# Encoder layer on one core: order of the first units, of the gates' rows and of two loads per head

## The chip, the cores and the metric

The kernel runs on 1 core of one Trainium2 chip. Times are device microseconds of that core for one execution of the whole program. TensorE's clock has two levels, 1.2 and 2.4 GHz; the profile gives the granted clock as a share of the higher one.

## The reference

One hybrid encoder layer on x of 1024 x 2048 (float32): RMSNorm, one input projection, eight heads of dilated sliding-window attention and four heads of a bidirectional mLSTM, gates, one output projection into the residual. Cut to what matters:

```python
h = _rmsnorm(x, norm_w)
proj = jnp.einsum('bsd,df->bsf', h, w_in)          # 2048 -> 8208 columns
q_a, k_a, v_a, z_a, q_m, k_m, v_m, o_m, z_m, g = jnp.split(proj, offsets, axis=-1)
qa = _rope_partial(_rmsnorm(q_a, q_norm_w), cos, sin)
ka = _rope_partial(_rmsnorm(k_a, k_norm_w), cos, sin)
# three (window, dilation) patterns per head, mixed by their softmax denominators
attn = dilated_attention(qa, ka, v_a) * jax.nn.silu(z_a)
# mLSTM forward and backward, with gates i, f from g; running-max stabiliser
h_fwd = _mlstm_chunkwise(qm, km, vm, i_fwd, jax.nn.log_sigmoid(f_fwd))
h_bwd = flip(_mlstm_chunkwise(flip(qm), flip(km), flip(vm), flip(i_bwd), flip(jax.nn.log_sigmoid(f_bwd))))
hm = jax.nn.sigmoid(o_m) * _rmsnorm(h_fwd + h_bwd, m_norm_w) * jax.nn.silu(z_m)
y = jnp.concatenate([attn, hm], axis=-1)
out = x + jnp.einsum('bsf,fd->bsd', y, w_out)
```

## The kernel before

The input projection is done by groups of 2 x 2 blocks with seven products instead of eight (a Strassen-Winograd scheme). A group takes one half of the 2048 inputs and a pair of column tiles; there are NG = 64 groups, so 448 units of one product each, then 128 units of the output projection. A product is 12 matmuls of 128 x 512: both sides are split into a rounded high half (float32r) and the rest as a low half, and high x high, low x high and high x low are added up in one PSUM bank.

The weights' side of a product is a block of w_raw or a sum s_tmp of blocks (s_one, s_two, s_three, s_four on VectorE). ScalarE rounds it (weight_hi, L978), VectorE subtracts to get the low half (weight_lo, L1214), two units ahead of TensorE. The x side are seven operands: B11, B21, B22 scaled by norm_w, and T1 = B12 - B11, T2 = B22 - T1, B22 - B12 (third sum) and B21 - T2 (fourth). They are built once for each of three stages, from four blocks of x in the arena: ScalarE casts the high half t_hi, VectorE makes the low half t_lo. For stage 0 this happens at the start of the program: x_block loads, scale_x on ScalarE, B11 scaled on VectorE after its low half, t_one and t_two on VectorE, t_three and t_four on GpSimd.

Each engine runs one list of instructions, in order, written as a loop over the units u; inside a unit every helper adds its part in a fixed order, and engines meet only by semaphores. On VectorE a unit is: softmax_dve of the heads, evict of the previous product, weight_lo of the block two units on, the x sums at the start, gates_and_norm, mlstm_dve, attention_dve, and the next group's weight sums. SyncE's list issues nearly all loads and stores; its waits stand in the same order, so a load waits behind the waits of the loads before it, among them those for s_done in next_weights. GpSimd's list issues the accumulating stores and the loads and stores of the turned rows (turned_rows).

The gates: in units 9 to 40 a small product is streamed, from unit 41 on VectorE turns it into rows (scans in units 53 to 55), and in units 59 to 64 it copies eight stripes of 32 x 1024 into rows, li and m. SyncE stores rows at unit 66, TensorE transposes at 67, ScalarE and VectorE read at 68 and 69. The first reader is the mLSTM; a wait for all of it stands at unit 92 in SyncE's list.

An attention head h starts at unit 357 + 18 h and spans some 26 units; "at" counts from its start. SyncE loads the raw q and k at -4, the quarter of rows that is rotated at 2, v at 4, the norms as broadcasts at 5 and 6, z at 6. VectorE rotates at 4 and 5, GpSimd stores the result to rot_dram and loads it back into the raw rows in another layout (4 to 6), VectorE waits for it and multiplies by the norms at 8 and 9 (normed, L1576). v is multiplied by xrs at 7 (L1624), z at 10 (L1621). TensorE makes scores from 10, transposes v at 11 and the first probabilities at 12 (L928); these wait for v's transposes having been copied out of PSUM, half by ScalarE, the rest by VectorE at 12 (L1649, L1652), the last statement of attention_dve. Heads 5 to 7 run mostly in the output units, where VectorE evicts a product by L1668.

Of the kernel before, what the change touches and what calls it, by code (L numbers as in the profile page):

```python
# [112 lines left out]
def build_program(nc, xT, w_all, w_gates, vecs, norm_cols, m_cols, att_mask, rope, eye, tri, fin, part, y_dram, t_dram, eps_dram, rows_dram, rs_dram,  # L113
                  rot_dram, outT):
    with ExitStack() as ctx:
# [270 lines left out]
        def _(sp):  # L386
# [46 lines left out]
            def gate_stores(u):  # L433
                if u == 48:
                    sp.wait_ge(x_cols, 7)
                    sp.dma_start(eps_dram, spread1[0:2 * TB, 0, :]).then_inc(rows_out, 16)
                if u == 66:
                    sp.wait_ge(g_dve, GD_ROWS)
                    for k in range(4):
                        sp.dma_start(rows_dram[k], rows[32 * k:32 * k + M_HEADS, :]).then_inc(rows_out, 16)  # L440
# [85 lines left out]
            def attention_loads(h, at):  # L526
# [38 lines left out]
                if at == 4:  # L565
                    if h > 0:
                        sp.wait_ge(a_pv, 4 * h)
                    tile_done(sp, g[0], 0)
                    sp.dma_start(halves(v_at), fin_tile(g[0], 0)).then_inc(v_raw, 16)
                if at == 6:  # L570
                    if h > 0:
                        sp.wait_ge(a_out, 16 * h)
                    tile_done(sp, g[1], 1)
                    sp.dma_start(halves(ystage), fin_tile(g[1], 1)).then_inc(z_raw, 16)
# [49 lines left out]
            for kt in range(KP):  # L624
                x_block(0, B11, kt)
            weights(0, 1, 0, 0)
            weights(0, 1, 1, 1)
            for kt in range(KP):
                x_block(0, B12, kt)
            weights(0, 0, 1, 4)  # L630
            for kt in range(KP):
                x_block(0, B22, kt)
# [70 lines left out]
        def _(pe):  # L703
# [64 lines left out]
            def gates_and_norm(u):  # L768
# [26 lines left out]
                if u == 67:  # L795
                    pe.wait_ge(g_dve, GD_ROWS)
                    for b in range(2 * TB):
                        src = (gr[3] if b < TB else gr[1])[0:64, (b % TB) * P:(b % TB + 1) * P]
                        t = nc.tensor.transpose(ps[:, 4 + b // TB, (b % TB) * 64:(b % TB + 1) * 64], src, ident[0:64, 0:64])
                    t.then_inc(g_pe, 1)  # L800
# [172 lines left out]
        def _(act):  # L973
# [19 lines left out]
            def scale_x(b, blk):  # L993
                for kt in range(KP):
                    if blk == B11:
                        act.wait_ge(b11_in[kt], 16 * (b + 1))
                    else:
                        act.wait_ge(b_in[blk], 16 * KP * (b + 1))
                    at = 8 * (b % 2) + 4 * (blk in (B21, B22)) + kt
                    nc.scalar.activation(stage[blk][:, kt, :], stage[blk][:, kt, :], ACT.Copy, scale=ncol[:, at:at + 1]  # L1000
                                         ).then_inc(pre[blk], 1)
# [30 lines left out]
            def gates_and_norm(u):  # L1032
# [30 lines left out]
                if u == 68:  # L1063
# [104 lines left out]
            for kt in range(KP):  # L1168
                act.wait_ge(b11_in[kt], 16)
                nc.scalar.activation(t_hi[:, 0, kt, :], stage[B11][:, kt, :], ACT.Copy, scale=ncol[:, kt:kt + 1]  # L1170
                                     ).then_inc(th_done[0], 1)
            weight_hi(1)
            scale_x(0, B12)
            for u in range(UNITS):
# [6 lines left out]
                if u == 0:  # L1181
                    scale_x(0, B22)
# [19 lines left out]
        def _(dve):  # L1202
# [133 lines left out]
            def gates_and_norm(u):  # L1336
# [75 lines left out]
                if u == 59:  # L1412
                    g_step(nc.vector.tensor_copy(rows[0:32, :], t[0:32, :]))
                if u == 60:
                    g_step(nc.vector.tensor_copy(rows[32:64, :], t[32:64, ::-1]))
                if u == 61:
                    g_step(nc.vector.tensor_copy(li[0:32, :], m[0:32, :]))
                    g_step(nc.vector.tensor_copy(li[32:64, :], m[32:64, ::-1]))
                if u == 62:
                    g_step(nc.vector.tensor_copy(m[0:32, :], f[0:32, :]))  # L1420
                    g_step(nc.vector.tensor_copy(m[32:64, :], f[32:64, ::-1]))
                if u == 63:
                    dve.wait_ge(g_act, 4)
                    g_step(nc.vector.tensor_copy(rows[64:96, :], wi[0:32, :]))
                if u == 64:
                    g_step(nc.vector.tensor_copy(rows[96:128, :], wi[32:64, ::-1]))
                    assert count[0] == GD_ROWS
                if u == 68:
# [4 lines left out]
                if u == 69:  # L1433
# [182 lines left out]
            def attention_dve(h, at):  # L1616
                if at in (4, 5):
                    rotate(h, at - 4)
                if at == 10:
                    dve.wait_ge(z_raw, 16 * (h + 1))  # L1620
                    nc.vector.tensor_tensor(ystage, ystage, xrs[:], ALU.mult).then_inc(a_zs, 1)  # L1621
                if at == 7:
# [49 lines left out]
            s_one(0)  # L1672
            s_two(0)
            s_three(0)
# [5 lines left out]
            weight_lo(1)  # L1680
            for kt in range(KP):
                dve.wait_ge(tl_done[0], kt + 1)
                nc.vector.tensor_scalar(stage[B11][:, kt, :], stage[B11][:, kt, :], ncol[:, kt:kt + 1], None, ALU.mult
                                        ).then_inc(pre[B11], 1)
            for kt in range(KP):
                t_one(0, kt)
            for u in range(UNITS):
# [6 lines left out]
                if u == 0:  # L1694
                    for kt in range(KP):
                        t_two(0, kt)
                    for kt in range(KP):
                        dve.wait_ge(th_done[1], kt + 1)
                        nc.vector.tensor_tensor(t_lo[:, 1, kt, :], t_src[1][:, kt, :],
                                                t_hi[:, 1, kt, :].bitcast(F32), ALU.subtract).then_inc(tl_done[1], 1)  # L1700
                if 1 <= u <= 5:
                    t_low(0, u + 1)
                if u == 6:
# [30 lines left out]
        def _(pool):  # L1734
            def t_three(b, kt):
                pool.wait_ge(t1_done, 4 * b + kt + 1)
                pool.wait_ge(pre[B22], 4 * b + kt + 1)
                nc.gpsimd.tensor_tensor(stage[B12][:, kt, :], stage[B22][:, kt, :], stage[B12][:, kt, :], ALU.subtract
                                        ).then_inc(t3_done, 1)

            def t_four(b, kt):
                pool.wait_ge(tl_done[2], t_made(2, b))
                pool.wait_ge(t2_done, 4 * b + kt + 1)
                nc.gpsimd.tensor_tensor(stage[B21][:, kt, :], stage[B21][:, kt, :], t2_at[:, kt, :], ALU.subtract
                                        ).then_inc(t4_done, 1)

# [32 lines left out]
            for u in range(UNITS):  # L1779
# [5 lines left out]
                if u == 0:  # L1785
                    for kt in range(KP):
                        t_three(0, kt)
                if u == 2:
                    for kt in range(KP):
                        t_four(0, kt)  # L1790
# [114 lines left out]
```

## Time and profile before

| | us |
|---|---|
| median of 3 runs | 2039.66 (2037.93 to 2040.56) |
| profiled execution | 2038.74 |
| its span | 2036.9 |
| TensorE busy | 1984.6 |
| VectorE busy | 1282.5 |
| ScalarE busy | 837.5 |
| GpSimd busy | 192.6 |
| mean granted clock | 0.996 |

The page's shares are means over stages: VectorE is at 63% over the span, but fuller in the first half. "Idle before" of a group names what ended the engine's wait. Positions in time are us from the start of the span.

### The profile page before, as it was taken

Reading aid. Unit: us, or ns where it says so; the run is one execution under the profiler, and the core shown is the slowest. Engines: PE = TensorE matmul, PEld = TensorE weight load, DVE = VectorE, ACT = ScalarE, POOL = GpSimd, SP = SyncE. Lnnn points to the kernel's source line nnn. Section 1 sums busy time; section 2 is a strip of 40 time slices with the busy share of each in tenths; the row PEclk is TensorE's granted clock in tenths of the full one; section 3 lists DMA queues with packets and bytes.
Section 4 is the critical chain, followed back from the end, with each engine's and each line's share of the span. In section 5 each row is a group of like instructions: output and inputs, shape, how many; then the busy total and the mean of one; then the engine's idle time right before and its main releaser. Section 6 shows DMA issues by size and latency. Waiting matters only on the chain.

```text
span 2036.9 us, 27050 instructions
## 1 busy us (share of the span) xinstructions
PE 1984.6 (97%) x9257; PEld 1623.8 (80%) x9257; DVE 1282.5 (63%) x2649; ACT 837.5 (41%) x1342; POOL 192.6 (9%) x188
## 2 busy tenths in 40 slices
PE   4999999899999999999999999999999999999999
PEld 3887788788888888888887878778777787788887
DVE  7777757768768768767766576575766544443222
ACT  5553325435435335334453343635537344251110
POOL 4340000110010010010000111010111000000000
PEclk8999999999999999999999999999999999999999
DMA  4673326474464365366457665364546625415443
GB/s 157 209 272 137 115 99 198 113 161 124 115 161 129 100 177 143 104 156 149 121 176 259 163 156 125 88 153 96 136 119 161 227 74 191 160 63 193 142 152 108
DMA packets 160231, 299.35 MB, mean 147 GB/s; under 512 B 17456, under 2 KB 36432, under 8 KB 157792
## 3 DMA queue, kind: packets, MB, share of 16 engines
q1 hardware_dynamic: 140128, 259.87, 38.8%
q0 software_dynamic: 19968, 37.76, 12.1%
q8 instruction: 75, 1.23, 0.3%
q14 instruction: 60, 0.49, 0.1%
HBM read 194.67 MB, written 102.90 MB: 146 GB/s over the span
## 4 chain that ended last, share of the span: by engine, by line
PE 88%; DVE 4%; DMA 3%; issue 3%; ACT 1%; SPq 0%; POOL 0%; DVEq 0%; ACTq 0%; POOLq 0%
PE ps L732 18%; PE ps L734 18%; PE ps L736 18%; PE ps L760 5%; PE ps L762 5%; PE ps L761 5%; PE ps L942 3%; PE ps L911 3%; PE ps L880 1%; PE ps L836 1%; PE ps L845 1%; PE ps L928 1%; DMA arena<-rot_dram 1%; PE ps L839 1%; PE ps L946 1%
## 5 line engine op out<-in xcount | busy, mean ns | idle before, releaser
L732 PE MATMUL ps<-t_hi,w_hi 128*128 128x512 f32 x1792 | 716.4, 400 | 42.2 <-DVE t_lo L1677 12.6
L734 PE MATMUL ps<-t_lo,w_hi 128*128 128x512 f32 x1792 | 701.5, 391 | 0.0
L736 PE MATMUL ps<-t_hi,w_lo 128*128 128x512 f32 x1792 | 701.1, 391 | 0.0
L732 PEld LDWEIGHTS ps<-t_hi,w_hi 128*128 128x128 f32 x1792 | 338.3, 189 | 123.6 <-issue 57.8
L736 PEld LDWEIGHTS ps<-t_hi,w_lo 128*128 128x128 f32 x1792 | 338.4, 189 | 72.0
L734 PEld LDWEIGHTS ps<-t_lo,w_hi 128*128 128x128 f32 x1792 | 338.9, 189 | 65.7
L978 ACT CAST w_hi<-w_raw 128x512 fp32r<-128x512 f32 x256 | 158.4, 619 | 391.4 <-PE ps L736 195.3
L1214 DVE TENSOR_TENSOR w_lo<-s_tmp,w_hi 128x512 fp32r<-128x512 f32 x256 | 182.4, 712 | 135.3 <-ACT w_hi L978 126.0
L1214 DVE TENSOR_TENSOR w_lo<-w_raw,w_hi 128x512 fp32r<-128x512 f32 x256 | 181.8, 710 | 133.9 <-ACT w_hi L978 127.5
L978 ACT CAST w_hi<-s_tmp 128x512 fp32r<-128x512 f32 x256 | 158.6, 619 | 239.9 <-PE ps L736 228.9
L760 PE MATMUL ps<-t_hi,w_hi 128*128 128x512 f32 x384 | 154.1, 401 | 5.5 <-DVE xt L1668 5.4
L762 PE MATMUL ps<-t_hi,w_lo 128*128 128x512 f32 x384 | 150.3, 391 | 0.0
L761 PE MATMUL ps<-t_lo,w_hi 128*128 128x512 f32 x384 | 150.2, 391 | 0.0
L1668 DVE TENSOR_TENSOR xt<-ps,s_tmp 128x512 f32<-128x512 f32 x64 | 44.0, 687 | 140.3 <-PE ps L762 140.3
L368 POOL DMA_DIRECT2D fin_dram<-xt x32 | 28.1, 878 | 877.1 <-ACT xt L991 858.4
L760 PEld LDWEIGHTS ps<-t_hi,w_hi 128*128 128x128 f32 x384 | 72.4, 188 | 26.6 <-issue 12.9
L1112 ACT ACTIVATE arena<-arena,mins 128x704 f32<-128x704 f32 x64 | 56.7, 886 | 81.2 <-DVE mins L1593 81.1
L762 PEld LDWEIGHTS ps<-t_hi,w_lo 128*128 128x128 f32 x384 | 72.4, 189 | 15.6
L761 PEld LDWEIGHTS ps<-t_lo,w_hi 128*128 128x128 f32 x384 | 72.5, 189 | 13.8
L1118 ACT ACTIVATE arena<-arena,sums 128x704 f32<-128x704 f32 x64 | 56.3, 880 | 63.5 <-DVE sums L1599 63.2
L1074 ACT ACTIVATE arena<-arena,g_cols 128x128 f32<-128x128 f32 x64 | 25.8, 403 | 131.3 <-DVE arena L1456 131.3
L986 ACT COPY xt<-ps 128x512 f32<-128x512 f32 x64 | 37.4, 585 | 89.7 <-PE ps L736 89.5
(217 smaller groups left out, 2657.0 us busy)
## 6 DMA issues: line engine op xcount, KB each, us to landing
w_raw<-w_all_dram SPq DMA_DIRECT2D x320, 256.0 KB, 3.8
fin_dram<-xt SPq DMA_DIRECT2D x128, 256.0 KB, 4.2
fin_dram<-xt POOLq DMA_DIRECT2D x128, 256.0 KB, 4.6
arena<-fin_dram SPq DMA_DIRECT2D x64, 512.0 KB, 7.3
arena<-xT_dram SPq DMA_DIRECT2D x44, 256.0 KB, 6.0
arena<-xT_dram SPq DMA_DIRECT2D x16, 512.0 KB, 4.3
arena<-rs_dram SPq DMA_DIRECT2D x16, 512.0 KB, 7.2
y_raw<-y_dram SPq DMA_DIRECT2D x16, 512.0 KB, 4.7
```

The lines of the kernel that those rows point to most:

```text
L732: nc.tensor.matmul(ps[:, bank, :], hi, t_hi[:, n, k, :], start=new and k == 0, stop=False, skip_group_check=True)
L734: nc.tensor.matmul(ps[:, bank, :], hi, t_lo[:, n, k, :], start=False, stop=False, skip_group_check=True)
L736: mm = nc.tensor.matmul(ps[:, bank, :], lo, t_hi[:, n, k, :], start=False, stop=k == KP - 1, skip_group_check=True)
L760: nc.tensor.matmul(ps[:, half, :], hi, yh, start=piece == 0 and k == 0, stop=False)
L761: nc.tensor.matmul(ps[:, half, :], hi, yl, start=False, stop=False)
L762: mm = nc.tensor.matmul(ps[:, half, :], lo, yh, start=False, stop=piece == 1 and k == KP - 1)
L911: nc.tensor.matmul(ps[:, 4, :], q, by_class(a_k)[:, :, h * P:(h + 1) * P], start=True, stop=True)
L942: nc.tensor.matmul(out, vtok[:, 4 * h + b, :], pT[:, b, :], start=b == 0, stop=False)
L978: nc.scalar.copy(w_hi[:, b % 3, :], src).then_inc(hi_done, 1)
L1112: nc.scalar.activation(prob[:, i % 2, 0:KEYS], prob[:, i % 2, 0:KEYS], ACT.Exp, bias=mins[:, i % 2:i % 2 + 1], scale=-1.0, accum_out=sums[ ...
L1118: nc.scalar.activation(prob[:, i % 2, 0:KEYS], prob[:, i % 2, 0:KEYS], ACT.Copy, scale=sums[:, 2 + i % 2:3 + i % 2]).then_inc(a_p, 1)
L1214: nc.vector.tensor_tensor(w_lo[:, b % 3, :], src, w_hi[:, b % 3, :].bitcast(F32), ALU.subtract).then_inc(lo_done, 1)
```

## The change

Three edits, none of which changes what is computed.

- First units: all four sums of x are on VectorE (t_three in unit 0, t_four in unit 2) and leave GpSimd. B11 is scaled by ScalarE, with B12, ahead of the second block's rounding; B22 is scaled before the loop. VectorE makes the low half of B11 first, then T1, and then the weight sums s_one and s_two; s_three goes into unit 0, behind the low half of T2. SyncE issues B12 before the two weight loads of slots 0 and 1, and B22 before that of slot 4.
- Gates' rows: the eight copies of units 59 to 64 go to units 61, 63, 66, 69, 72 and 74; store, transposes, reads and the last product of units 66 to 69 go to 76 to 79.
- Heads: SyncE loads v at 7 instead of 4 and z at 9 instead of 6; VectorE multiplies v at 10 instead of 7, z at 12 instead of 10.

```diff
-                if u == 66:
+                if u == 76:
                     sp.wait_ge(g_dve, GD_ROWS)
-                if at == 4:
+                if at == 7:
                     if h > 0:
                         sp.wait_ge(a_pv, 4 * h)
...
-                if at == 6:
+                if at == 9:
                     if h > 0:
                         sp.wait_ge(a_out, 16 * h)
...
             for kt in range(KP):
                 x_block(0, B11, kt)
+            for kt in range(KP):
+                x_block(0, B12, kt)
             weights(0, 1, 0, 0)
             weights(0, 1, 1, 1)
             for kt in range(KP):
-                x_block(0, B12, kt)
+                x_block(0, B22, kt)
             weights(0, 0, 1, 4)
-            for kt in range(KP):
-                x_block(0, B22, kt)
...
+                    if (b, blk) == (0, B11):
+                        act.wait_ge(tl_done[0], kt + 1)
...
+            scale_x(0, B11)
+            scale_x(0, B12)
             weight_hi(1)
-            scale_x(0, B12)
+            scale_x(0, B22)
...
                 if u == 0:
-                    scale_x(0, B22)
...
-                if u == 59:
+                if u == 61:
                     g_step(nc.vector.tensor_copy(rows[0:32, :], t[0:32, :]))
-                if u == 60:
+                if u == 63:
...
-                if at == 10:
+                if at == 12:
                     dve.wait_ge(z_raw, 16 * (h + 1))
...
-                if at == 7:
+                if at == 10:
                     dve.wait_ge(v_raw, 16 * (h + 1))
...
             weight_lo(0)
-            s_one(0)
-            s_two(0)
-            s_three(0)
...
-            weight_lo(1)
-            for kt in range(KP):
-                dve.wait_ge(tl_done[0], kt + 1)
-                nc.vector.tensor_scalar(stage[B11][:, kt, :], stage[B11][:, kt, :], ncol[:, kt:kt + 1], None, ALU.mult
-                                        ).then_inc(pre[B11], 1)
             for kt in range(KP):
                 t_one(0, kt)
+            s_one(0)
+            s_two(0)
+            weight_lo(1)
...
+                    s_three(0)
+                    for kt in range(KP):
+                        t_three(0, kt)
                 if 1 <= u <= 5:
                     t_low(0, u + 1)
+                if u == 2:
+                    for kt in range(KP):
+                        t_four(0, kt)
...
-                if u == 0:
-                    for kt in range(KP):
-                        t_three(0, kt)
-                if u == 2:
-                    for kt in range(KP):
-                        t_four(0, kt)
                 squares(u)
```

## Rows read from the trace of the kernel before

**Rows 1.** The page, part 1: busy us and share of the span.

```profile
PE 1984.6 (97%) x9257; PEld 1623.8 (80%) x9257; DVE 1282.5 (63%) x2649; ACT 837.5 (41%) x1342; POOL 192.6 (9%) x188
```

**Rows 2.** TensorE's waits: us in total, times, longest.

```profile
PE ps L732 <- DVE t_lo L1305: 9.2, 5, 2.9
...
PE ps L760 <- DVE xt L1668: 5.4, 3, 2.2
```

**Rows 3.** Timeline, 0 to 45 us: start, duration, instruction, idle before and releaser.

```profile
7.49 1.35 ACT L1170 ACTIVATE t_hi<-arena,ncol 128x512 fp32r<-128x512 f32 x2 [0.30 <-DMA arena<-xT_dram]
9.67 0.69 DVE L1249 TENSOR_TENSOR s_tmp<-w_raw 128x512 f32<-128x512 f32 x1 [2.88 <-DMA w_raw<-w_all_dram]
...
12.56 0.77 PE L732 MATMUL ps<-t_hi,w_hi 128*128 128x512 f32 x1 [12.56 <-DVE t_lo L1677]
...
12.80 2.56 ACT L1000 ACTIVATE arena<-arena,ncol 128x512 f32<-128x512 f32 x4 [1.00 <-DMA arena<-xT_dram]
...
14.93 1.67 DVE L1683 TENSOR_SCALAR arena<-arena,ncol 128x512 f32<-128x512 f32 x4
...
17.28 14.65 POOL L1738 TENSOR_TENSOR arena<-arena 128x512 f32<-128x512 f32 x4 [16.83 <-DVE arena L1276]
...
19.52 2.49 DVE L1282 TENSOR_TENSOR arena<-arena 128x512 f32<-128x512 f32 x4
...
22.76 0.77 PE L732 MATMUL ps<-t_hi,w_hi 128*128 128x512 f32 x1 [4.98 <-DVE t_lo L1699]
...
23.04 0.62 ACT L978 CAST w_hi<-s_tmp 128x512 fp32r<-128x512 f32 x1
...
26.16 1.90 ACT L1022 CAST t_hi<-arena 128x2048 fp32r<-128x2048 f32 x1
...
28.09 2.71 DVE L1305 TENSOR_TENSOR t_lo<-arena,t_hi 128x2048 fp32r<-128x2048 f32 x1 [3.07 <-ACT t_hi L1022]
...
30.94 0.70 PE L732 MATMUL ps<-t_hi,w_hi 128*128 128x512 f32 x1 [2.95 <-DVE t_lo L1305]
...
36.94 1.77 DVE L1270 TENSOR_TENSOR s_tmp<-w_raw,s_tmp 128x512 f32<-128x512 f32 x1
...
40.33 2.28 DVE L1305 TENSOR_TENSOR t_lo<-arena,t_hi 128x2048 fp32r<-128x2048 f32 x1
...
42.75 0.47 PE L732 MATMUL ps<-t_hi,w_hi 128*128 128x512 f32 x1 [2.59 <-DVE t_lo L1305]
```

**Rows 4.** Window 212 to 234 us: PE, PEld, DVE, ACT, POOL busy; clock, DMA share, GB/s.

```profile
212.20:234.00 21.80, 21.80 (x98) 18.02 (x97) 20.59 (x37) 7.75 (x13) 0.00 (x0) 1.00 0.40 134
```

**Rows 5.** Line L1621; then the timeline at the first transposes of heads 0 and 3.

```profile
L1621 DVE TENSOR_TENSOR arena<-arena,xrs x8: 1207/1215/1232, 1193.5 to 1778.1; 128x1024 f32<-128x1024 f32 x8
...
1203.85 0.63 PE L928 MATMUL ps<-ident,arena 128*128 128x128 f32 x4 [0.26 <-DVE arena L1652]
...
1450.11 0.41 DVE L1652 COPY arena<-ps 64x256 f32<-64x256 f32 x1
...
1450.66 0.52 PE L928 MATMUL ps<-ident,arena 128*128 128x128 f32 x3
```

**Rows 6.** Lines L1576 and L1776; queue in 1590 to 1608; timeline of heads; clock in 1522.

```profile
  DMA arena<-rot_dram: 25.0, 10
...
DMA to landing us min/median/max: 2.8/5.2/7.7
...
q1 hardware_dynamic: 2362, 5.35, 91.8%
...
1521.94 0.47 PE L732 MATMUL ps<-t_hi,w_hi 128*128 128x512 f32 x1 [2.51 <-DVE xt L1232]
...
1602.67 2.04 DVE L1576 SCALAR_TENSOR_TENSOR arena<-arena,spare 128x1024 f32<-128x1024 f32 x1 [6.13 <-DMA arena<-rot_dram]
...
1773.94 0.47 PE L760 MATMUL ps<-t_hi,w_hi 128*128 128x512 f32 x1 [2.23 <-DVE xt L1668]
...
1522.00:1526.00 4.00, 4.00 (x11) 3.13 (x12) 3.67 (x5) 0.00 (x0) 0.00 (x0) 0.58 0.09 15
```

More of the change, by code:

```diff
@@ L794, in gates_and_norm @@
                     t.then_inc(x_pe, 1)
-                if u == 67:
+                if u == 77:
                     pe.wait_ge(g_dve, GD_ROWS)
@@ L1062, in gates_and_norm @@
                     nc.scalar.activation(gr[5][0:64, :], gr[5][0:64, :], ACT.Exp).then_inc(g_act, 1)
-                if u == 68:
+                if u == 78:
                     act.wait_ge(g_pe, 1)
@@ L1411, in gates_and_norm @@
                     assert count[0] == GD_INTER
-                if u == 59:
+                if u == 61:
                     g_step(nc.vector.tensor_copy(rows[0:32, :], t[0:32, :]))
-                if u == 60:
+                if u == 63:
                     g_step(nc.vector.tensor_copy(rows[32:64, :], t[32:64, ::-1]))
-                if u == 61:
+                if u == 66:
                     g_step(nc.vector.tensor_copy(li[0:32, :], m[0:32, :]))
                     g_step(nc.vector.tensor_copy(li[32:64, :], m[32:64, ::-1]))
-                if u == 62:
+                if u == 69:
                     g_step(nc.vector.tensor_copy(m[0:32, :], f[0:32, :]))
                     g_step(nc.vector.tensor_copy(m[32:64, :], f[32:64, ::-1]))
-                if u == 63:
+                if u == 72:
                     dve.wait_ge(g_act, 4)
                     g_step(nc.vector.tensor_copy(rows[64:96, :], wi[0:32, :]))
-                if u == 64:
+                if u == 74:
                     g_step(nc.vector.tensor_copy(rows[96:128, :], wi[32:64, ::-1]))
                     assert count[0] == GD_ROWS
-                if u == 68:
+                if u == 78:
                     dve.wait_ge(g_pe, 1)
@@ L1432, in gates_and_norm @@
                         g_step(nc.vector.tensor_copy(g_cols[:, :, d, :], src))
-                if u == 69:
+                if u == 79:
                     dve.wait_ge(g_act, 6)
@@ L1734, in _ @@
         def _(pool):
[L1735 to L1745, printed above, removed]
             def added(g, n):
```

## The prediction

> **What bounds the kernel now.** I read the page's first part, then who TensorE waited for, then the order of time around each wait. TensorE is busy for 1984.6 us of a span of 2036.9 us [rows 1], so a gain can only come out of its 52.3 us of idle time and out of stretches at the lower clock level. The waits [rows 2] and the order of time [rows 3] put the largest part, 26.8 us, in the first units (12.56, 4.98, 2.95 and four smaller ones, all for low halves t_lo of x). The rest is in the gates' stage, at the changes of stage, and in single waits of the attention stage, 5.4 of them in the output units. After the start, every microsecond that VectorE keeps TensorE waiting is lost in full, and one that it doesn't is worth nothing. The profiled execution took 2038.74 us, 1.84 us more than its span and 0.92 us under the median of 2039.66; I sum against 2038.74.
>
> **Part 1, the first units.** Before [rows 3]: TensorE starts at 12.56 because VectorE made three sums of weights, from 9.67, after a wait of 2.88 for w_raw, ahead of t_lo of B11. It starts product 1 at 22.76, product 2 at 30.94, product 3 at 37.16, product 4 at 42.75. I redo each chain with the durations of these rows.
>
> Product 0 starts early: two of ScalarE's four casts of B11 are done before 7.49, and VectorE can follow them at once, so TensorE starts about 7.6 instead of 12.56. With 12 matmuls at the lower clock level (0.427 us apart) it ends near 12.7. This wins nothing unless product 1 also moves.
>
> Product 1 needs T2 = B22 - T1. In the new order ScalarE scales B11 (from 7.49 + 1.35 = 8.84, in 2.56 like B12's four, to 11.4), then to 14.0 B12, which landed at 12.8 and now is two loads of 256 KB earlier, 0.8 us each (its own four landed from 9.67 to 12.80), near 11.3. VectorE's last T1 then starts at 14.0, and its two sums of weights come only behind it: 14.6 and, 0.8 later by its dependence on the first, 15.4. ScalarE, in order, rounds these weights at 16.1, scales B22 from 16.7 to 19.25 and rounds block 2; VectorE answers with the low half at 19.95 and T2 at 20.6, where it stood at 19.52. TensorE follows 3.24 later, as before (22.76 - 19.52): product 1 at **23.85, 1.1 late**.
>
> Product 2: block 3 takes the third sum of weights, which now runs behind T2 and t_lo (20.6 + 2 x 2.41 = 25.4), so ScalarE rounds block 3 at 26.1 instead of 23.04. Behind it wait the scaling of B21 (2.56) and the cast of B21 (1.90, at 26.16 before, now 29.3 to 31.2). VectorE's low half takes 2.28 instead of 2.71, product 2 starts at 33.6, **2.7 late**.
>
> Here the second half of the edit pays. GpSimd's two sums, 14.65 us for four instructions in the first row, go to VectorE at 0.62 each (the four of L1282 take 2.49): 8 x 0.62 = 5.0 us more work, of which the first 2.5 lie in a wait for ScalarE (28.5 to 31.2). In return 4 x 0.42 = 1.7 us of scaling leave it, and the slow instructions beside GpSimd end: the weight sum at 36.94 took 1.77 us where its like takes 0.69. So the low half for product 3 is there near 37 (33.4 evict, 34.0 low weights, 34.6 + 2.28), and product 3 starts when product 2 ends. After an idle stretch of 4.9 us product 2 runs at the lower of the two levels (1.2 instead of 2.4 GHz, 0.427 us between matmuls instead of 0.228), as the matmuls after 12.56, 22.76 and 30.94 did, 12 x 0.427 = 5.1 at most; it ends at 38.3, **1.1 late**. From there ScalarE's evict, rounding and cast take 2.95, the low half 2.28: product 4 at 43.85, against 42.75, and the next ones follow at VectorE's pace of 4.0 us (one low half of x, one sum or evict each) as before. The idle time ahead of product 4 is 2.8 us; one of 2.59 before kept the higher level [rows 3], one of 2.51 elsewhere was followed by a clock of 0.58 [rows 6]. So part of 1.6 us (8 x 0.2) may come on top. I take **+1.3 us**, bounds -2 (product 2 only 0.5 late, no lower clock) and +4 (all links late and one more stretch of lower clock). The loads of the next group's weights, which SyncE issues after the third sum, go out at 26.2 instead of 13.3; their first reader is at 44, so 0, and 2 to 3 us if another load stood in front.
>
> **Part 2, the gates' rows.** Eight copies of 0.68 us move from units 59 to 64 to units 61 to 74, with the stores, transposes and reads 10 units later. TensorE waited 0.6 to 1.2 us per unit up to 211.8, behind the scans of units 53 to 55, which don't move; in 212 to 234, where the copies stand, it was busy for 21.80 of 21.80 us [rows 4]. The copies are hidden already: **0**. After 234 VectorE has gaps of 2 us a unit for 1.4 us of copies, and the first reader of the results is at unit 92. Lower bound -0.5 (a little less backlog), upper +1.
>
> **Part 3, v and z of a head.** Two effects of opposite sign.
> (a) Multiplying z by xrs, 1.21 us [rows 5], moves from at=10 to at=12, where attention_dve has it directly ahead of the two copies of vtok and vedge for which the first transposes of probabilities on TensorE wait. v takes its place at 10, at equal cost, and its reader (L893) stands behind scores that wait for VectorE's unit 11, so that is free. In head 0 TensorE already idled 0.26 for the last copy; in head 3 that copy ends at 1450.11 + 0.41 and L928 starts 0.14 later, at 1450.66: no slack [rows 5]. Of the same rows for the eight heads the slack is 0, 0.1, 0, 0, 0.5 and, in the output stage, 2.0, 2.7 and 2.7. The insertion costs 1.15 (1.21 less the overlap of 0.06 of neighbours): 1.15 + 1.05 + 1.15 + 1.15 + 0.65 = **+5.2 us**. Bounds 3.5 and 5.8.
> (b) The gain: VectorE stood 25.0 us in 10 waits for the rotated rows (L1576), up to 6.13, and TensorE behind it 0.9 in head 0, 2.51 in head 4, 2.23 in head 7 [rows 6] and twice, 3.2 together, in head 5 (with head 7's the 5.4 of [rows 2]), 8.9 us; after heads 4 and 7 the clock also fell (0.58 in 1522 to 1526), 1.6 us each. All 12 are the ceiling. GpSimd stores the turned rows and loads them back; a load took 2.8 to 7.7 us (median 5.2) [rows 6], beside SyncE's 512 KB loads. In head 5 (1590 to 1608) SyncE moved 5.35 MB in 18 us, 0.3 MB a us, so one of these is 1.7 us. v was issued just before GpSimd's first store there, z just after the second. With both behind, the first round trip should shrink by some 1.4, the second by 2.6, which takes up 2.9 of the 3.2. Head 7 likewise (2.23 to some 0.8, and no lower clock), head 0 wholly. But head 4: SyncE's loads are tied by program order to VectorE's sums of weights, and there v falls where z was issued before, so its 2.51 stays, and z then stands ahead of the second round trip; in head 2 both come behind one such gate, 0.4 worse. I take 0.9 + 2.9 + 3.0 - 0.2 - 0.4, some **-6 us**, bounds 0 and -10.
>
> By the Trainium skill ("DMA: Bandwidth & Descriptors", Queues, rings and completion order) each DMA engine takes turns between the queues that have work. The depth of SyncE's queue then wouldn't matter to GpSimd's transfer as long as it isn't empty, and (b) would be near 0: the sum would be +6.5. No row here isolates it; the spread of 2.8 to 7.7 us speaks for some effect of load, and I leave it a chance (R1).
>
> **Sum**: 2038.74 + 1.3 + 0 + 5.2 - 6.0 = 2039.2; I give **2039.5**, rounded toward the median.
>
> **Rivals.**
> R1, slower: the round trips of the rotated rows stay as long as they are, because SyncE's queue is never empty in them (v and z move behind, other 512 KB broadcasts and weights fill in). Then only the z instruction's cost remains: 2038.74 + 1.3 + 5.2 = 2045.2. It decides as soon as (b) is under 2.4 us in all. For it: in 1590 to 1608 SyncE's queue took 91.8% of the DMA engines' time with 5.35 MB [rows 6], of which v and z are 1 MB. Against: 2.8 us was possible for one load. Chance 0.22.
> R2, faster: v and z were what held the round trips; the waits in heads 0, 4, 5, 7 and the clock falls vanish (-12), with z's cost of 5.2 and the start's 1.3: 2033.2. If also z's instruction finds slack because VectorE reaches unit 12 earlier (it lost 1.2 us of work at unit 7), 2029. For it: VectorE's waits are the longest of the stage. Against: head 4's order of issue. Chance 0.13.
> R3, faster at the start: TensorE's start 5 us earlier carries through, and without GpSimd the chain of the x sums shortens by its 3 us of slow instructions: 2034 with the rest at zero. Against: the chain goes through ScalarE, in order, and two of its links (weight sums behind T1, third sum behind t_lo) get longer. Chance 0.06.
> The forecast itself, within 4.1 us: 0.59 of the cases.
>
> **Range and chances.** A run of this kernel tells 0.2% (4.1 us) from no change. Parts 1 and 3 may each be off by 2 to 5 us: 2034.0 to 2046.0 leaves out under 2 in 10, R2's better half and what is beyond R1. Faster by over 0.2% 0.17, within 0.2% 0.61, slower 0.22.
>
> **What the changed profile would show.** TensorE's first matmul near 7.6, product 1 near 23.9, product 2 near 33.6, product 4 near 43.9, and at ScalarE a wait of 2 us for the third weight sum; no idle time in 212 to 260 as before; L928 released by the vedge copy with 0.3 to 1.4 us of idle in heads 0 to 4; the waits of L1576 under 25 us by some 10, and TensorE's 5.4 us of L1668 mostly gone, the 2.51 not. I am wrong if products 2 to 4 are on time or early, if L928 doesn't wait, or if the round trips haven't changed.

## The result

| | before | changed |
|---|---|---|
| median | 2039.66 | 2047.59 |
| lowest and highest | 2037.93 to 2045.14 | 2047.01 to 2053.24 |
| profiled execution | 2038.74 | 2051.75 |
| its span | 2036.9 | 2049.9 |

The ratio is 1.004, with a 95% interval of 1.003 to 1.005: 8 us slower. The time lies above the stated range of 2034.0 to 2046.0. Of the cases of the prediction R1 (2045.2) is the nearest. The profiled execution is 13 us over the one of before, 5 us more than the medians are apart: it lies 4.2 above its own median, the one of before 0.9 below. A part of these 5 is explained under the clock below.

The page of the changed kernel has nearly the busy times of [rows 1]; only GpSimd lost its eight sums. TensorE's busy time grew by 3.1 us, its idle time by 9.9:

```profile
PE 1987.7 (97%) x9257; PEld 1625.9 (79%) x9257; DVE 1283.6 (63%) x2653; ACT 839.7 (41%) x1346; POOL 170.0 (8%) x180
```

So the difference is again mostly in what TensorE waited for. The same view as [rows 2], of the changed kernel (lines moved by 3 on VectorE: L1305 is L1308, L1668 is L1671, L1652 is L1655):

```profile
PE ps L732 <- DVE t_lo L1697: 12.1, 1, 12.1
PE ps L732 <- DVE t_lo L1308: 9.9, 3, 5.0
PE ps L732 <- DVE t_lo L1677: 7.6, 1, 7.6
PE ps L760 <- DVE xt L1671: 6.8, 4, 3.3
PE ps L928 <- DVE arena L1655: 6.0, 5, 1.7
...
PE ps L911 <- DVE arena L1579: 2.7, 2, 2.0
```

The reader sees four things: the first wait went from 12.6 to 7.6 while the one of product 1 went from 5.0 to 12.1; L928, 0.3 us in one wait before, now has 6.0 us in five; the waits behind the rotated rows in the output units, 5.4 before, are 6.8; and the scores (L911) wait 2.7 us for the multiplication by the norms (L1579), for which they did not wait before. The timeline of the first units, in the columns of [rows 3]:

```profile
7.60 0.77 PE L732 MATMUL ps<-t_hi,w_hi 128*128 128x512 f32 x1 [7.60 <-DVE t_lo L1677]
...
14.72 0.69 DVE L1279 TENSOR_TENSOR arena<-arena 128x512 f32<-128x512 f32 x1
15.33 0.68 DVE L1252 TENSOR_TENSOR s_tmp<-w_raw 128x512 f32<-128x512 f32 x1
...
21.14 2.49 DVE L1285 TENSOR_TENSOR arena<-arena 128x512 f32<-128x512 f32 x4
...
24.38 0.77 PE L732 MATMUL ps<-t_hi,w_hi 128*128 128x512 f32 x1 [12.11 <-DVE t_lo L1697]
...
26.68 0.62 ACT L978 CAST w_hi<-s_tmp 128x512 fp32r<-128x512 f32 x1 [1.91 <-DVE s_tmp L1266]
...
34.16 0.77 PE L732 MATMUL ps<-t_hi,w_hi 128*128 128x512 f32 x1 [4.97 <-DVE t_lo L1308]
...
44.61 0.47 PE L732 MATMUL ps<-t_hi,w_hi 128*128 128x512 f32 x1 [2.71 <-DVE t_lo L1308]
```

Products 0, 1, 2 and 4 stand at 7.60, 24.38, 34.16 and 44.61, where the prediction had 7.6, 23.85, 33.6 and 43.85, and the kernel before 12.56, 22.76, 30.94 and 42.75. The gates' stage, behind the late products that follow the scans, as [rows 4]:

```profile
217.20:240.00 22.80, 22.80 (x103) 18.85 (x102) 17.93 (x31) 8.23 (x13) 0.00 (x0) 1.00 0.45 148
235.00:275.00 40.00, 40.00 (x188) 33.03 (x187) 25.58 (x39) 11.49 (x20) 0.00 (x0) 1.00 0.38 123
```

TensorE is busy all the time, as before. In head 0, z's multiplication (L1624) is followed by the two copies and the last of them releases L928, as in [rows 5], but 1.68 us of idle time instead of 0.26:

```profile
1208.59 1.22 DVE L1624 TENSOR_TENSOR arena<-arena,xrs 128x1024 f32<-128x1024 f32 x1
1209.72 0.69 DVE L1652 COPY arena<-ps 128x512 f32<-128x512 f32 x1
1210.32 0.41 DVE L1655 COPY arena<-ps 64x256 f32<-64x256 f32 x1
...
1210.88 0.63 PE L928 MATMUL ps<-ident,arena 128*128 128x128 f32 x4 [1.68 <-DVE arena L1655]
```

And the rotated rows, as [rows 6]: the waits of L1579 (L1576 before) and the landing of the turned rows' loads, then head 5.

```profile
  DMA arena<-rot_dram: 32.1, 9
...
DMA to landing us min/median/max: 2.6/6.3/10.2
...
1600.54 0.57 POOL L1763 DMA_DIRECT2D rot_dram<-arena  x1 [13.15 <-DVE arena L1572]
...
1604.82 0.76 SPq L569 DMA_DIRECT2D arena<-fin_dram  x1
1606.54 0.40 SPq L574 DMA_DIRECT2D arena<-fin_dram  x1
1607.81 0.56 POOL L1768 DMA_DIRECT2D arena<-rot_dram  x1 [3.76 <-DMA rot_dram<-arena]
...
1614.05 2.03 DVE L1579 SCALAR_TENSOR_TENSOR arena<-arena,spare 128x1024 f32<-128x1024 f32 x1 [9.66 <-DMA arena<-rot_dram]
...
1616.83 0.47 PE L760 MATMUL ps<-t_hi,w_hi 128*128 128x512 f32 x1 [3.30 <-DVE xt L1671]
```

VectorE waited 32.1 us for them instead of 25.0. In head 5 the loads of v and z (L569, L574) go out right ahead of the turned rows' load (L1768), which then takes 6.2 us until VectorE goes on; TensorE's wait is 3.30 where two waits had made 3.2. The same head before, with VectorE going on at 1602.67 [rows 6]:

```profile
1590.92 0.57 POOL L1771 DMA_DIRECT2D rot_dram<-arena  x1 [13.15 <-DVE arena L1569]
...
1597.39 0.56 POOL L1776 DMA_DIRECT2D arena<-rot_dram  x1 [2.96 <-DMA rot_dram<-arena]
```

From the issue of the first store to the issue of its load back it was 6.5 us and is 7.3, and from there to VectorE 5.3 and 6.2: the first round trip of head 5 got 1.8 us longer.

### The profile page after: what moved, and what is told of

Its sections match the earlier page's. It is cut to its first block, busy times and chain, and to the rows that moved or that the text cites. A ratio compares the mean times of both kernels' runs of the same rounds, so it can differ in the third digit from the quotient of the medians.

```text
span 2049.9 us, 27055 instructions
## 1 busy us (share of the span) xinstructions
PE 1987.7 (97%) x9257; PEld 1625.9 (79%) x9257; DVE 1283.6 (63%) x2653; ACT 839.7 (41%) x1346; POOL 170.0 (8%) x180
## 3 DMA queue, kind: packets, MB, share of 16 engines
q0 software_dynamic: 19968, 37.76, 12.1%
## 4 chain that ended last, share of the span: by engine, by line
PE 85%; DVE 5%; issue 4%; DMA 3%; ACT 2%; SPq 0%; POOL 0%; DVEq 0%; ACTq 0%; POOLq 0%
PE ps L732 18%; PE ps L736 18%; PE ps L734 18%; PE ps L760 5%; PE ps L761 5%; PE ps L762 5%; PE ps L942 3%; PE ps L911 2%; PE ps L880 1%; PE ps L928 1%; PE ps L836 1%; PE ps L845 1%; DMA arena<-rot_dram 1%; PE ps L839 1%; PE ps L946 1%
## 5 line engine op out<-in xcount | busy, mean ns | idle before, releaser
L732 PE MATMUL ps<-t_hi,w_hi 128*128 128x512 f32 x1792 | 717.5, 400 | 42.0 <-DVE t_lo L1697 12.1
L760 PE MATMUL ps<-t_hi,w_hi 128*128 128x512 f32 x384 | 154.0, 401 | 6.8 <-DVE xt L1671 6.8
L1671 DVE TENSOR_TENSOR xt<-ps,s_tmp 128x512 f32<-128x512 f32 x64 | 44.0, 687 | 142.1 <-PE ps L762 142.1
L760 PEld LDWEIGHTS ps<-t_hi,w_hi 128*128 128x128 f32 x384 | 72.4, 189 | 27.7 <-issue 13.6
```

The source lines that it names most:

```text
L732: nc.tensor.matmul(ps[:, bank, :], hi, t_hi[:, n, k, :], start=new and k == 0, stop=False, skip_group_check=True)
L760: nc.tensor.matmul(ps[:, half, :], hi, yh, start=piece == 0 and k == 0, stop=False)
L1671: nc.vector.tensor_tensor(xt[:, e % 6, :], ps[:, e % 2, :], s_tmp[:, e % 3, :], ALU.add).then_inc(o_done, 1)
```

## The experiments

**One part at a time.** My theory after the result: the start costs 2 us and some of the clock, the rows nothing, z's place 5 to 6 us, and the later loads give nothing back. The rival for each part is in its expectation. e1_start has the first units' edit alone, e2_rows the gates' rows alone, e3_heads the heads' edit alone; these are whole parts of the diff shown above. e4_mults has only the multiplications of v and z moved:

```diff
-                if at == 10:
+                if at == 12:
                     dve.wait_ge(z_raw, 16 * (h + 1))
...
-                if at == 7:
+                if at == 10:
                     dve.wait_ge(v_raw, 16 * (h + 1))
```

> The kernel before with the first units' edit alone (x sums on VectorE, new order, DMA order). Theory (the forecast's chain, corrected by the profile of after): products 1, 2 and 4 start near 24.4, 34.2 and 44.6 us as in the changed kernel, the chain is 1.9 us late there, and every later fall of the clock adds 1.6 us: 2041.5 to 2045, with the profile of after (5.0 us late at 200 us) at the upper end. Rival (the start edit pays because TensorE starts 5 us earlier and GpSimd is out of the way): at or under 2038.

> The kernel before with the gates' rows spread over units 61 to 79 alone. Theory: the copies were hidden, so no change, within 1 us of before, and TensorE idles the same 0.6 to 1.2 us before four products near 200 to 212 us and nowhere else up to 350. Rival: the spread steps meet other work of VectorE and cost TensorE 1 to 3 us between 235 and 270 us.

> The kernel before with the heads' edit alone: v loaded at 7, z at 9, multiplied at 10 and 12. Theory (rival R1 of the prediction): L928 waits for the vedge copy in heads 0 to 4, 5.7 us in all, and the waits for the rotated rows don't shrink: 2044 to 2048. The forecast's theory: the round trips shrink and give 6 us back: 2039.

> The kernel before with only VectorE's multiplications moved (v at 10, z at 12), the loads at 4 and 6 as before. If the whole loss of the heads' edit is the z instruction ahead of the vtok and vedge copies: as e3_heads, +5 to +6 us, 2044 to 2046, and L928 waits in heads 0 to 4. If the later loads cost something of their own (v and z among the turned rows' loads): e3_heads is 1 to 4 us slower than this one. If they pay: e3_heads is faster than this one.

Measured, against the kernel before in the same rounds (its median there 2041.39). The kernel before was timed again with every group of runs, and its median moved between 2040.51 and 2041.64. So kernels of different groups are compared by their ratios to it, and not by their medians:

| | median | ratio | 95% interval |
|---|---|---|---|
| e1_start | 2043.86 | 1.0009 | 0.9998 to 1.0021 |
| e2_rows | 2040.66 | 0.9999 | 0.9989 to 1.0010 |
| e3_heads | 2047.57 | 1.0031 | 1.0021 to 1.0040 |
| e4_mults | 2047.94 | 1.0028 | 1.0015 to 1.0042 |

The three parts add up to 1.0039, and the whole is 1.004: no loss in their meeting is seen. The start costs some 2 us (0.0009 x 2040) by these times, with an interval from -0.4 to 4.3 that includes zero; the rows cost nothing, give or take 2 us. The heads' edit is the loss, and e4_mults, in which no load is moved, has nearly all of it. The waits of TensorE in e3_heads, then in e4_mults:

```profile
PE ps L928 <- DVE arena L1652: 7.0, 5, 1.7
PE ps L760 <- DVE xt L1668: 6.6, 4, 3.3
```

```profile
PE ps L760 <- DVE xt L1668: 6.4, 5, 2.1
PE ps L928 <- DVE arena L1652: 5.0, 5, 1.4
```

e4_mults also tells where VectorE's longer waits for the rotated rows come from. The waits of L1576 in it, with no load moved:

```profile
  DMA arena<-rot_dram: 30.3, 8
```

They are 21.0 to 26.5 us in six profiles that leave the heads as before, and 29.1 to 32.1 in the four with the later loads. The multiplication of v has left unit 7, VectorE reaches unit 8 earlier and stands there longer. This part of the wait costs nothing by itself, for it doesn't change when the rows come.

**The place of z's multiplication.** e5_z_behind is e3_heads with the instruction moved behind the two copies of the same unit; e14_after_z_behind is the same edit on the changed kernel.

```diff
             def attention_dve(h, at):
-                if at == 12:
-                    dve.wait_ge(z_raw, 16 * (h + 1))
-                    nc.vector.tensor_tensor(ystage, ystage, xrs[:], ALU.mult).then_inc(a_zs, 1)
...
                                           ps[0:CLASSES * EDGE, 6, 0:256].rearrange("p (h d) -> p h d", d=P)
                                           ).then_inc(a_vd, 1)
+                if at == 12:
+                    dve.wait_ge(z_raw, 16 * (h + 1))
+                    nc.vector.tensor_tensor(ystage, ystage, xrs[:], ALU.mult).then_inc(a_zs, 1)
```

> The heads' edit alone, as e3_heads, but z's multiplication stands behind the copies of vtok and vedge in unit 12, not ahead of them. Theory (the loss of the heads' edit is that instruction's place): L928's waits fall from 7.0 us to under 1, and the kernel is 5 to 6 us faster than e3_heads (2047.6), within 2 us of before. Rival (the loss is spread over the stage, by DMAs or by VectorE's load in units 10 to 13): it stays 3 us or more slower than before.

> The changed kernel with z's multiplication behind the copies of vtok and vedge in unit 12, not ahead. Theory: 5 to 6 us faster than the changed kernel (2047.6), so 2041 to 2043, that is 1 to 2 us over before, what the start edit alone showed. Rival (the edits hurt each other): it stays over 2045.

e5_z_behind: 2041.30, ratio 1.0006 (0.9995 to 1.0018), beside 2040.57 for before; e3_heads had 1.0031. L928's waits for the last copy (L1649 there) fell from 7.0 to this:

```profile
PE ps L928 <- DVE arena L1649: 0.8, 2, 0.5
```

e14_after_z_behind: 2043.86, ratio 1.0014 (1.0003 to 1.0024), where the changed kernel has 1.004. The gain is 2.5 thousandths in the one and 2.6 in the other, 5.1 and 5.3 us of 2040, as expected. Its median lies 0.9 us above the expected 2041 to 2043, but its rounds' before was at 2041.64, and by the ratio it is 2.9 us over before. The place of one instruction is the larger part of the result. e5_z_behind is also the most direct measure of the later loads: it has them, without the cost of z's place, and it is 1.2 us slower than before, with an interval from -1.0 to 3.7.

**What the rotated rows wait for.** Each of these kernels leaves work out. e6_thin_vz loads only 8 of 128 partitions of v and z, at the places of before; e13_thin_norms_alone does that to the two broadcasts of the norms; e9_thin_norms to all four.

```diff
-                    sp.dma_start(halves(v_at), fin_tile(g[0], 0)).then_inc(v_raw, 16)
+                    sp.dma_start(halves(v_at)[0:8], fin_tile(g[0], 0)[0:8]).then_inc(v_raw, 16)
...
-                    sp.dma_start((a_q, a_k)[i], rs_dram[h, i].rearrange("r b n -> (r b n)").unsqueeze(0)
-                                 .to_broadcast([P, SEQ])).then_inc(bc_in[i], 16)
+                    sp.dma_start((a_q, a_k)[i][0:8], rs_dram[h, i].rearrange("r b n -> (r b n)").unsqueeze(0)
+                                 .to_broadcast([8, SEQ])).then_inc(bc_in[i], 16)
```

> The kernel before, with the loads of v and z of every head cut to 8 of their 128 partitions (the rest of v and z keeps stale values, so attention's values and gate are not computed rightly; all instructions and waits stay). This takes 1 MB a head out of SyncE's queue. Forecast's theory (v and z lengthen the turned rows' round trips by 1.4 to 2.6 us): L1576's waits fall from 25 us to 10 or less, TensorE's waits in heads 0, 4, 5 and 7 nearly vanish, 2030 to 2035. Rival (the round trips don't depend on them, because the engines take turns between queues, or because other loads fill in): L1576's waits stay above 18 us and the time within 2 us of before.

> As e6_thin_vz (v and z loads cut to 8 partitions), and the two broadcasts of the norms, 512 KB each, cut to 8 of 128 partitions too: attention is not computed rightly. Now 2 MB a head are out of SyncE's queue. If SyncE's queue sets the turned rows' round trips at all, L1576's waits fall well under e6's 23.7 us, to 10 or less, and a load's median from 5.2 to under 4 us; the time falls 3 to 6 us under before. If the round trips are GpSimd's own (its queue with the accumulating stores, its issue, four transfers one behind the other), the waits stay above 18 us.

> The kernel before with only the two broadcasts of the norms cut to 8 of 128 partitions (q and k are not normalised rightly), v and z loaded in full at 4 and 6. If the broadcasts are what the turned rows meet: most of e9's gain, 2029 to 2032. If only both together matter: 2035 to 2039. If the later loads of the change could only have worked with the broadcasts gone, this run has L1576's waits between e9's 16.8 and 25 us and few waits of TensorE behind them.

The interval of the changed kernel is from its own rounds, the others from theirs.

| | median | ratio | 95% interval | turned rows, store / load, median us |
|---|---|---|---|---|
| before | 2040.6 | 1 | | 5.4 / 5.2 |
| changed | 2047.59 | 1.004 | 1.003 to 1.005 | 4.7 / 6.3 |
| e6_thin_vz | 2039.13 | 0.9992 | 0.9983 to 1.0001 | 3.7 / 5.2 |
| e13_thin_norms_alone | 2034.55 | 0.9960 | 0.9946 to 0.9973 | 3.9 / 5.7 |
| e9_thin_norms | 2029.13 | 0.9948 | 0.9934 to 0.9963 | 3.2 / 4.6 |

The waits of L1576 in e6_thin_vz, e13_thin_norms_alone and e9_thin_norms:

```profile
  DMA arena<-rot_dram: 23.7, 7
```

```profile
  DMA arena<-rot_dram: 18.5, 6
```

```profile
  DMA arena<-rot_dram: 16.8, 4
```

Taking 15/16 of v and z away is worth 1.6 us, with an interval from -0.2 to 3.5; the forecast wanted 6 from only moving them, and of e6's two cases the rival came true. Thinned, v and z shorten the stores from 5.4 to 3.7, but not the loads, which set the end. The broadcasts alone are worth 8 us (5.5 to 11), between the two cases of their expectation, and both together 10.6 (7.5 to 13.5); that both are worth more than the broadcasts alone isn't shown, since the intervals meet. So SyncE's traffic does lengthen the stage, and the broadcasts are its weightier part, but even with both gone 16.8 of 25.0 us of VectorE's waits stay. e9's waits were expected at 10 or less if SyncE's queue set them, and over 18 if it didn't; it is between, so neither theory was right alone. How the broadcasts act isn't settled: TensorE's waits for L1668 are 6.5 us in the profile of e13, no less than before, while those for L1232 are 1.9 instead of 4.0; that profile (2039.56) is the slowest of its six executions, 5 us over their median. I didn't separate the rotated rows from the broadcasts' own landing.

**The round trip against its distance.** e7_rotate_early leaves all loads and gives the rotated rows one unit more.

```diff
-                if at in (4, 5):
-                    rotate(h, at - 4)
+                if at in (3, 4):
+                    rotate(h, at - 3)
...
-                if at in (4, 5):
-                    i = at - 4
+                if at in (3, 4):
+                    i = at - 3
                     pool.wait_ge(a_rot, 8 * h + 4 * i + 4)
...
-                if at in (5, 6):
-                    i = at - 5
+                if at in (4, 5):
+                    i = at - 4
```

> The kernel before with the rotation and its store and load one unit earlier (VectorE and GpSimd at 3 and 4, load back at 4 and 5), loads of v and z untouched. Theory (the rotated rows' round trip of about 11 us against four units is what VectorE waits for): the waits of L1576 fall from 25 us to under 10, TensorE's 2.5 in head 4, 3.2 in head 5 and 2.2 in head 7 mostly vanish with their clock falls: 2030 to 2035. Rival (the wait moves on to the broadcasts of the norms, or into unit 3 where VectorE gets 1.8 us more): within 2 us of before.

2035.07, ratio 0.9977 (0.9966 to 0.9987). A load took longer than before (median 6.0 for 5.2), the store was shorter (3.0 for 5.4), and VectorE no longer waited for them; TensorE's waits for L1668 fell from 5.4 to 2.6 us. What was left at L1576, 8.3 us, is the broadcast of the norms:

```profile
  DMA arena<-rs_dram: 8.3, 6
```

So the theory came true. Of its rival, the other releaser was there, but with a smaller wait, and the time it wanted (within 2 us of before) was not.

**The start.** e8_start_new keeps the x sums on VectorE and t_lo of B11 first, but puts the weight sums right behind it and leaves ScalarE's and SyncE's lists as before. e11_early_t also has the cast and the low half ahead of the evict in units 2 to 5.

```diff
             weight_lo(0)
-            s_one(0)
-            s_two(0)
-            s_three(0)
             for kt in range(KP):
                 dve.wait_ge(th_done[0], kt + 1)
...
+            s_one(0)
+            s_two(0)
+            s_three(0)
...
             for u in range(UNITS):
...
+                if 2 <= u <= 5:
+                    t_low(0, u + 1)
                 if 1 <= u <= IN_UNITS:
                     evict(u - 1)
```

> The kernel before with the x sums on VectorE and t_lo of B11 first, but with the three weight sums right behind it, DMA order and ScalarE's order as before, B11 scaled on VectorE before the second block's low half. Theory (what hurts the start edit is the place of the weight sums and of ScalarE's scalings, not the move off GpSimd): product 1 starts near 20.5 instead of 22.8, product 4 near 39 to 40 instead of 42.75, 2 to 4 us faster than before. Rival (the sums on VectorE are what makes the start late): product 4 at or behind 42.75.

> e8_start_new, and in units 2 to 5 the cast and the low half of the next x operand stand ahead of the evict and the weights' steps on ScalarE and VectorE. Theory (what is left of the start is ScalarE's list: the cast for product 4 waits behind an evict that waits for product 2, and the 2.7 us of idle time there bring the low clock back): no idle time over 1.5 us after product 2, no fall of the clock after 35 us, 2 to 4 us faster than e8_start_new. Rival (VectorE's 4 us a unit sets the pace anyway): within 1 us of e8_start_new.

e8_start_new: 2037.19, ratio 0.9987 (0.9978 to 0.9996). e11_early_t: 2035.38, ratio 0.9977 (0.9967 to 0.9988); the two intervals meet, so the second step is not shown by the times alone. The profiles speak for it: TensorE reaches its first wait behind a scan of the gates at 199.49 in e8_start_new, and at 194.75 and 194.92 in the two kernels with the early casts, e11_early_t and e12_all. The timeline of e8_start_new and of e11_early_t:

```profile
20.75 0.77 PE L732 MATMUL ps<-t_hi,w_hi 128*128 128x512 f32 x1 [7.97 <-DVE t_lo L1699]
28.89 0.62 PE L732 MATMUL ps<-t_hi,w_hi 128*128 128x512 f32 x1 [2.88 <-DVE t_lo L1305]
38.89 0.47 PE L732 MATMUL ps<-t_hi,w_hi 128*128 128x512 f32 x1 [2.71 <-DVE t_lo L1305]
48.47 0.47 PE L732 MATMUL ps<-t_hi,w_hi 128*128 128x512 f32 x1 [2.28 <-DVE t_lo L1305]
```

```profile
28.30 0.47 PE L732 MATMUL ps<-t_hi,w_hi 128*128 128x512 f32 x1 [2.85 <-DVE t_lo L1307]
36.91 0.47 PE L732 MATMUL ps<-t_hi,w_hi 128*128 128x512 f32 x1 [1.28 <-DVE t_lo L1307]
```

Product 1 at 20.75 instead of 24.38 with the same sums on VectorE: the move off GpSimd is sound, and the loss lay in what e8_start_new leaves out, the places of the weight sums, of the scalings and of SyncE's loads. No run parts these three. With the casts early no idle time over 1.3 us is left behind product 2 in the first units.

**The gates' heavy steps, and all together.** e10_scans also spreads the steps ahead of the rows.

```diff
-                if u in (54, 55):
-                    for c in range(4 * (u - 54), 4 * (u - 54) + 4):
+                if u in (56, 58):
+                    for c in range(2 * (u - 56), 2 * (u - 56) + 4):
```

> The gates' rows spread as in e2_rows, and the steps ahead of them too: the scans of units 54 and 55 go to 56 and 58, the next steps to 59, 61 and 63, the exponential to 64, the copies to 65 to 74. Theory (the 3.7 us of TensorE's idle time at 200 to 212 come from three heavy VectorE steps in a row, not from the copies): 2 to 3.7 us faster than before, idle time of 0.8 behind the first scan stays at most. Rival: the load only moves, within 1 us of before.

> e7_rotate_early, e10_scans and e11_early_t together. If their gains lie in different stages and add up (4.7 from e7, 2.7 from e8, 2 to 4 each from the scans and the early casts): 2026 to 2031. If the clock's falls move with the phase of the work and take part of it back: 2031 to 2035.

e10_scans: 2037.88, ratio 0.9989 (0.9978 to 1.0000). Of the four waits of TensorE at 200 to 212 two are left:

```profile
199.62 0.47 PE L732 MATMUL ps<-t_hi,w_hi 128*128 128x512 f32 x1 [0.78 <-DVE xt L1232]
203.73 0.47 PE L732 MATMUL ps<-t_hi,w_hi 128*128 128x512 f32 x1 [1.12 <-DVE xt L1235]
```

e12_all (e7, e10 and e11 together): **2026.62**, ratio 0.9935 (0.9923 to 0.9947). It is 13 us faster than the kernel before and 21 faster than the changed one. The single gains make 4.7 + 2.2 + 4.7 = 11.6 us (the ratios x 2040), the whole 13.3 with 2.4 either way; within that they add up.

## Why the prediction was wrong

**What bounds the kernel** held: TensorE issues the same 9257 instructions in both, and the difference is its idle time and its clock.

**Part 1** held in its chain, and was too small in size. The links came 0.5 to 0.8 us later than forecast (24.38 for 23.85, 44.61 for 43.85; the last sum, 38.3 + 2.95 + 2.28, makes 43.5 and not the 43.85 written). +1.3 was forecast; e1_start's times give 1.8 (-0.4 to 4.3), and the profiles 3.8, as told under the clock below. Both lie inside -2 to +4. Of the lower clock the text counted "part of 1.6", and all three profiles of this start have twice 1.6. The wait of ScalarE for the third weight sum is there with 1.91 us (2 forecast). R3 fell: TensorE's start 5 us earlier was worth nothing.

**Part 2** held: 0 forecast, -0.2 with 2 us either way measured.

**Part 3 (a)** held: +5.2 forecast. L928 waits in exactly the five heads of the list, 6.0 us in the profile of the changed kernel; e4_mults measured 5.7 (3.1 to 8.6), and taking the instruction out of the way gave 5.1 back.

**Part 3 (b)** is the step that failed: -6 us forecast for moving the loads of v and z behind the round trips, nothing measured. e3_heads against e4_mults (1.0031 and 1.0028) gives +0.6 for the later loads, 3.4 either way, and e5_z_behind against the kernel before +1.2 (-1.0 to 3.7). I priced the whole round trip by the megabytes in SyncE's queue, 1.7 us for each 512 KB, and took 1.4 and 2.6 us off. Two things were wrong in this.

First, what the store wins the load loses. In the seven profiles with nothing thinned, v and z loaded at their old places and the rotation at its old one, the median store takes 5.0 to 5.8 us and the median load back 5.2 to 5.5; in the four with the later loads it is 4.2 to 4.7 and 5.8 to 6.3. By the order of issue v and z had been beside the store and now are beside the load. The text saw this for heads 2 and 4 only; in head 5, where it took 2.9 us off, the first round trip got 1.8 us longer. Second, v and z were never the main part: cutting them to a sixteenth gave 1.6 us. R1, with a chance of 0.22, had this case, (b) near zero.

The rule of the Trainium skill ("DMA: Bandwidth & Descriptors", Queues, rings and completion order) that each DMA engine takes turns between the queues that have work pointed to R1's side. The loads' unchanged 5.2 us in e6_thin_vz agree with it; the stores' 3.7 instead of 5.4 there, and the shift from store to load above, don't fit "doesn't matter at all", and no run here isolates it.

**The rest of the miss.** With (b) at zero the sum is 2045.2; the median is 2.4 above. Part 1 with the 3.8 us of the profiles instead of 1.3 would fill this, but 2.4 us is also within what the times leave open for each part. The upper end of 2046.0 was 1.6 too low, though it was meant to hold R1: I had put R1's point value at it, and not R1's own spread from the start and from (a).

## What to carry to other kernels

Before an instruction is moved to a later unit, look at what stands right behind it there and who waits for that: 1.2 us of VectorE ahead of a copy that TensorE waits for cost 5 us over five heads, and behind that copy nothing that the times show. A transfer that comes too late is better started a step earlier (4.7 us) than made faster by moving its neighbours away (0), unless a run with the neighbours thinned has shown first that they are what it waits for. In the first units, an early start of the bottleneck engine is worth nothing while the second operand's chain through another engine's ordered list gets longer. And a longer wait of an engine that isn't the bottleneck (VectorE's 30.3 us for 25.0 in e4_mults) need not mean that what it waits for got slower: look first whether it only arrives earlier.

## What the runs showed of the hardware

**The clock.** Stretches of lower clock came and went with the same instructions. In e7_rotate_early the first units are those of the kernel before, and product 4 starts at 42.81, after 2.61 us of idle time; before it was 42.75 after 2.59 [rows 3]. The windows of 40 to 60 us of before and of e7_rotate_early, and the next product after a wait in the latter:

```profile
40.00:60.00 20.00, 15.37 (x66) 12.01 (x66) 16.26 (x20) 10.68 (x11) 0.00 (x0) 1.00 0.61 207
```

```profile
40.00:60.00 20.00, 15.15 (x52) 11.72 (x52) 14.61 (x17) 8.20 (x8) 0.00 (x0) 0.83 0.56 182
...
52.38 0.47 PE L732 MATMUL ps<-t_hi,w_hi 128*128 128x512 f32 x1 [2.24 <-DVE t_lo L1305]
```

The granted clock is 1.00 in the one and 0.83 in the other, and product 6 starts at 52.38 instead of 50.76. The changed kernel's profiled execution had the same 0.83 there:

```profile
40.00:60.00 20.00, 15.04 (x52) 11.52 (x51) 14.94 (x17) 8.99 (x9) 0.00 (x0) 0.83 0.49 148
```

It reaches the gates' stage 5.0 us late (its first wait behind a scan is at 204.82, before at 199.85), of which product 4 shows 1.9; two stretches at the lower level, behind products 4 and 6, make the rest, at 1.6 each (8 matmuls at 0.427 instead of 0.228 us apart).

One profile of each kernel is too little here, and it is the one of before that was lucky. Ten profiles have its first units (before, e2, e3, e4, e5, e6, e7, e9, e10, e13). The clock in their windows of 40 to 60 us is 0.99 or 1.00 in five, 0.91 in two and 0.83 in three, and the first wait behind a scan comes between 199.62 and 203.02, at 200.95 on average. The three with the new start (changed, e1, e14) all have 0.83, and the wait at 204.82, 204.48 and 205.02. So the new start costs 3.8 us by the profiles; the timed runs of e1_start, 1.8 with an interval from -0.4 to 4.3, allow it. Of the 5 us by which the two first profiles overstate the loss, 1.1 is the luck of before. The rest is behind 205 us: the changed kernel's profile has 2.7 us at L911 and 6.8 at L760, where e14_after_z_behind, which differs only in z's place, has none and 4.8.

An idle time of about 2 us is thus a risk, not a price. The same 2.6 us ahead of product 4 kept the higher level in one execution and lost it in another, and the level also fell around a wait of 1.92 us (e10_scans, ahead of product 3 at 36.95). Behind the waits of 1.28 us and less that follow product 2 in e11_early_t it stayed at 1.00.

**GpSimd's sums.** The same sum of 128 x 512 took 0.62 us a piece on VectorE and 14.65 us for four on GpSimd while both engines worked [rows 3], and with them gone VectorE's weight sum of 1.77, which had stood beside the second of these groups of four (7.96 us), took 0.69.
